# FoX attention in a one-core layer kernel: the small products of a step gathered at one place, the lists of ScalarE and VectorE reordered

## The chip, the cores and the metric

The kernel runs on one core of a Trainium2 chip. A core has five engines that matter here, each with an instruction list of its own that it works through strictly in order: TensorE (PE in the profile, with its weight loader PEld), VectorE (DVE), ScalarE (ACT), GpSimd (POOL) and SyncE (SP), which issues DMA transfers. They wait for one another by semaphores. The metric is the device time of one execution in microseconds (us); the median of three executions before the change is 911.9 us.

## The reference

One layer of a decoder over 528 tokens (16 meta tokens and 512 of the sequence), 1024 features. Cut to what matters:

```python
hn = rms_norm(h_res, norm_mix_gain)
part = lambda i: hn @ w_in[:, o[i]:o[i + 1]]       # q, k, v, fg, glu (2x), gate_attn, gate_conv
# attention, 16 heads of 64, query blocks of 128 that see the keys up to their end:
s = q_block @ k.T / 8 + cum[t] - cum[s]            # cum: running sum of log_sigmoid(fg)
p = softmax(where(causal, s, -inf))
a = (p @ v) @ w_attn_out
# convolution branch:
u = glu[:D] * sigmoid(glu[D:])
c = causal_depthwise_conv(u, conv_dw_w, conv_dw_b)  # 31 taps
c = silu(layer_norm(c)) @ w_conv_out + b_conv_out   # layer_norm over the features
h_res = h_res + (sigmoid(gate_attn) * a + sigmoid(gate_conv) * c) @ w_out
# then a squared-ReLU MLP of 4096 and a last rms_norm; meta tokens are dropped
```

## The kernel before

**Products in three parts.** Every matrix product is done with numbers split in a high and a low part (`w_hi`, `w_lo`, and the same for the input), as three products: high x high, low x high, high x low. A weight chunk is 128 output features times 1024 inputs. SyncE loads it into `raw`, ScalarE copies the high part (`high`, L577), VectorE subtracts to get the low part (`low`, L955), and TensorE runs 24 products of 512 columns (or 24 pairs of 2 x 264 columns where all 528 tokens are wanted, L1451) in `chunk`. There are two places for split chunks, so `low(c + 1)` has to be done before chunk c + 1 starts.

**Pairs of heads.** The stage around the change goes through the projections of q, k, v and the gates, four chunks for each of 8 pairs of heads. It is a loop over k, of 8 steps s = 0 to 7; step s is one half chunk, that is 12 products. In step s of loop k TensorE multiplies the weights of pair k, and beside that does attention for pair k - 1: 8 units, unit s = 4 h + q, for head h of the pair and query block q, with 144, 272, 400 or 528 keys. For a unit the work goes round the engines:

- TensorE: scores S (`unit_scores`, L1571 and L1572), two short products (four for q = 3).
- VectorE: `row_least` (L1091) adds the mask to the scores in PSUM, writes `prob` and finds the row's least value; ScalarE: `exponential` (L666) with the row sum; VectorE: `sum_reciprocal` (L1097); ScalarE: `normalise` (L674).
- TensorE: the transpositions T of P (`unit_transpose`, L1585), q + 2 tiles of 128 x 128 into PSUM. It waits for `normalise` of the unit (`s_pn`) and for all earlier units' `probs_low` (`s_ptl`).
- ScalarE `probs_high` (L682) and VectorE `probs_low` (L1103) take the two parts of the turned P out of PSUM; in the code these calls stand in `turned_out` and `turned_low`, which in step s handle unit s - 2, and in steps 0 and 1 units 6 and 7 of the pair before.
- TensorE: `half_out` (P times v, L1602 and L1605) for two query blocks at once. Then `out_copy` (L689) and `out_high` (L693) on ScalarE, `out_add` (L1110) and `out_low` (L1114) on VectorE. Once a pair TensorE turns v (`values_transpose`, L1613), followed by `values_high` (L735) and `values_low` (L1148).

The evacuations of the projections on ScalarE are in `projection_out` and `second_copy`, on VectorE in `projection_low` (L1141: steps 4 and 6 for the low parts of q and k). VectorE also works off the convolution as single taps of 128 x 512 (`tap`, L1051): the tables `TAPS_FIRST_PAIR` and `TAPS_STEP` say how many taps each of the 8 steps has, and `taps(s, k, a, b)` does those from the a-th to before the b-th of its step. GpSimd adds a finished convolution row to the sum over features (`add_conv`, L552), once the scores of unit 5 are done, in the third to the eighth pair, and at the end twice more, with two memsets (L564, L565) ahead of the last.

**What sets the order.** All lists are written out by hand. In TensorE's `pair_step` the tuple `CUTS` says after how many of the 12 products the small work is put in: S(s) after 4; v's transpositions (step 2) after 7; T(s - 1) after 11, followed by `half_out` in steps 1, 3, 5 and 7.

**The tail.** The loop k = 9 has only the last units and the gates' chunks, together with the layer norm of the convolution: ScalarE and VectorE split the sum over the features (`sum_parts`, L818 and L1248), TensorE's `spread` (L1620, L1621) multiplies both parts with `mean_w` to lay the mean over all partitions, ScalarE copies it to `bc` (L824), VectorE subtracts it from the 8 rows (L1257), ScalarE squares (L829) and VectorE sums the squares (L1239).

## Time and profile before

| what | value |
|---|---|
| runs | 911.46, 911.90, 912.39 us, median 911.90 |
| profiled execution, its own time | 911.48 us |
| its span (first to last instruction) | 909.5 us |
| PE busy | 900.1 us, 99% |
| PEld busy | 784.2 us, 86% |
| DVE busy | 614.1 us, 68% |
| ACT busy | 445.0 us, 49% |
| POOL busy | 22.3 us, 2% |
| mean granted clock of TensorE | 0.999 |
| share of the chain that ended last | PE 92%, DVE 4%, ACT 2%, others 3% |

The profile is of one execution. Its own time is 2.0 us longer than its span, which is what lies before the first and after the last instruction. The pairs of heads take about 134 to 405 us of the span. The shares of busy time are means over the whole span, so a stage has to be looked at by itself: VectorE's 68% are some 95% in the pairs and under half in the MLP. The chain that ended last gives 41% and 17% to the chunk's products (L1455, L1451), 19% to the MLP's (L1707), and 3% each to the transpositions of P and to one form of P times v.

### The profile page before, as it was taken

The numbers are of one execution on the slowest core, as the hardware profiler recorded it, in microseconds if no ns is written. First come the engines' busy times: TensorE is split into PE (matmuls) and PEld (weight loads), VectorE is DVE, ScalarE is ACT, GpSimd is POOL, SyncE is SP. The second block draws the span as 40 slices with busy tenths as digits, with TensorE's granted clock in tenths as the row PEclk, the third lists the DMA queues.
The fourth block names the chain that finished last, engine by engine and source line by source line (L and its number), as shares of the span: only waits on it lengthen the run. The fifth ranks groups of instructions, "written<-read, shape, count | busy, mean of one in ns | idle before, by whom it ended". The sixth has DMA issues, their size and how long they took to land.

```text
span 909.5 us, 13686 instructions
## 1 busy us (share of the span) xinstructions
PE 900.1 (99%) x5039; PEld 784.2 (86%) x5039; DVE 614.1 (68%) x959; ACT 445.0 (49%) x722; POOL 22.3 (2%) x40
## 2 busy tenths in 40 slices
PE   8999999999999999999999999999999999999997
PEld 7999999899999999888888888888888888888886
DVE  7799989999999999987765444533443354334543
ACT  6532246777778777766843244421243133214523
POOL 2010000000000000010000000000000000000000
PEclk9999999999999999999999999999999999999999
DMA  9333332212221222213323532323233333333602
GB/s 267 93 98 92 92 93 70 70 49 70 70 68 48 70 70 54 81 52 92 116 82 104 186 92 85 101 94 100 87 100 108 92 92 92 115 93 98 179 1 93
DMA packets 129466, 84.34 MB, mean 93 GB/s; under 512 B 3103, under 2 KB 118815, under 8 KB 129424
## 3 DMA queue, kind: packets, MB, share of 16 engines
q1 hardware_dynamic: 128192, 82.32, 31.1%
q10 hardware_dynamic: 640, 1.18, 0.4%
q8 instruction: 25, 0.41, 0.2%
q0 software_dynamic: 592, 0.29, 0.2%
q14 instruction: 17, 0.14, 0.1%
HBM read 81.62 MB, written 2.16 MB: 92 GB/s over the span
## 4 chain that ended last, share of the span: by engine, by line
PE 92%; DVE 4%; ACT 2%; issue 1%; DMA 1%; SPq 0%; ACTq 0%
PE pj L1455 41%; PE pQ L1707 19%; PE pj L1451 17%; PE pQ L1585 3%; PE pQ L1602 3%; PE pj L1773 2%; PE pQ L1773 2%; PE pj L1493 1%; DVE cv L1051 1%; PE pQ L1572 1%; PE pQ L1571 1%; DVE w_lo L955 1%; DMA ga<-in_x_dram 1%; ACT w_hi L577 1%; PE pQ L1605 1%
## 5 line engine op out<-in xcount | busy, mean ns | idle before, releaser
L955 DVE TENSOR_TENSOR w_lo<-raw,w_hi 128x1024 fp32r<-128x1024 f32 x129 | 157.6, 1222 | 113.5 <-ACT w_hi L577 113.2
L577 ACT ACTIVATE w_hi<-raw 128x1024 fp32r<-128x1024 f32 x129 | 135.9, 1053 | 161.5 <-PE pQ L1707 121.3
L1455 PE MATMUL pj<-in_hi,w_lo 128*128 128x512 f32 x512 | 201.5, 394 | 0.0
L1455 PE MATMUL pj<-in_lo,w_hi 128*128 128x512 f32 x512 | 200.6, 392 | 0.0
L1455 PE MATMUL pj<-in_hi,w_hi 128*128 128x512 f32 x512 | 200.1, 391 | 0.2 <-DVE w_lo L955 0.2
L1051 DVE SCALAR_TENSOR_TENSOR cv<-u,prm,cv 128x512 f32<-128x512 f32 x240 | 170.6, 745 | 0.5
L1455 PEld LDWEIGHTS pj<-in_hi,w_hi 128*128 128x128 f32 x512 | 96.3, 188 | 19.5 <-DVE w_lo L955 0.6
L1455 PEld LDWEIGHTS pj<-in_lo,w_hi 128*128 128x128 f32 x512 | 96.2, 188 | 17.8
L1455 PEld LDWEIGHTS pj<-in_hi,w_lo 128*128 128x128 f32 x512 | 96.3, 188 | 17.2
L1707 PE MATMUL pQ<-w_hi,mid_hi 128*128 128x512 f32 x256 | 99.8, 390 | 0.0
L1707 PE MATMUL pQ<-w_lo,mid_hi 128*128 128x512 f32 x256 | 99.6, 389 | 0.0
L1707 PE MATMUL pQ<-w_hi,mid_lo 128*128 128x512 f32 x256 | 99.6, 389 | 0.0
L1451 PE MATMUL pj<-in_hi,w_lo 128*128 128x264 f32 x480 | 97.9, 285 | 0.0
L1451 PE MATMUL pj<-in_lo,w_hi 128*128 128x264 f32 x480 | 97.4, 284 | 0.0
L1451 PE MATMUL pj<-in_hi,w_hi 128*128 128x264 f32 x480 | 96.7, 283 | 0.0
L1451 PEld LDWEIGHTS pj<-in_hi,w_hi 128*128 128x128 f32 x480 | 75.1, 188 | 1.0 <-DVE w_lo L955 0.3
L1451 PEld LDWEIGHTS pj<-in_lo,w_hi 128*128 128x128 f32 x480 | 74.1, 188 | 0.0
L1451 PEld LDWEIGHTS pj<-in_hi,w_lo 128*128 128x128 f32 x480 | 74.0, 188 | 0.0
L898 ACT ACTIVATE prob<-pT 128x512 f32<-128x512 f32 x32 | 20.2, 632 | 101.7 <-DVE pT L1348 101.7
L1707 PEld LDWEIGHTS pQ<-w_hi,mid_hi 128*128 128x128 f32 x256 | 48.1, 188 | 10.0
L1707 PEld LDWEIGHTS pQ<-w_hi,mid_lo 128*128 128x128 f32 x256 | 48.1, 188 | 9.9
L1707 PEld LDWEIGHTS pQ<-w_lo,mid_hi 128*128 128x128 f32 x256 | 48.1, 188 | 9.9
(206 smaller groups left out, 1226.1 us busy)
## 6 DMA issues: line engine op xcount, KB each, us to landing
raw<-in_w_in_dram SPq DMA_DIRECT2D x57, 512.0 KB, 3.8
raw<-in_w_mlp_up_dram SPq DMA_DIRECT2D x32, 512.0 KB, 4.0
raw<-in_w_mlp_down_dram SPq DMA_DIRECT2D x32, 512.0 KB, 3.8
raw<-in_w_attn_out_dram SPq DMA_DIRECT2D x8, 512.0 KB, 3.6
raw<-in_w_conv_out_dram SPq DMA_DIRECT2D x8, 512.0 KB, 3.6
raw<-in_w_out_dram SPq DMA_DIRECT2D x8, 512.0 KB, 3.9
ga<-in_x_dram SPq DMA_DIRECT2D x4, 512.0 KB, 8.4
cv<-in_x_dram SPq DMA_DIRECT2D x1, 2048.0 KB, 9.1
```

The costliest lines, as they stand in the source:

```text
L577: A(w_hi[:, c % SPLIT, :], raw[:, c % RAW, :], ACT.Copy).then_inc(s_hi, 1)
L898: A(scratch(j), pT[:, j % 2, :], ACT.Square).then_inc(s_hf, 1)
L955: V.tensor_tensor(w_lo[:, c % SPLIT, :], raw[:, c % RAW, :], w_hi[:, c % SPLIT, :].bitcast(F32), ALU.subtract).then_inc(s_lo, 1)
L1051: V.scalar_tensor_tensor(out=dst, in0=src, scalar=par(j, m), in1=dst, op0=ALU.mult, op1=ALU.add).then_inc(s_conv, 1)
L1451: last = mm(prod(c, T)[:, h * HALF:(h + 1) * HALF], wt, src[:, kt * ROW + FIRST + h * HALF:kt * ROW + FIRST + (h + 1) * HALF], **flags)
L1455: last = mm(prod(c), wt, src[:, at:at + NT], **flags)
L1493: last = mm(prod(c, T)[:, h * HALF:(h + 1) * HALF], (w_hi, w_hi, w_lo)[what][:, c % SPLIT, kt * P:(kt + 1) * P], (in_hi, in_lo, in_hi)[wha ...
L1571: mm(dst[:, a:b], q_a[:, k % 2, h, q * P:(q + 1) * P], k_a[:, k % 2, h, a:b], start=True, stop=False)
L1585: last = nc.tensor.transpose(turned(q)[:, t * P:(t + 1) * P], probs(q, t * P, (t + 1) * P), ident[:, :])
L1602: last = mm(dst.rearrange("p (c n) -> p c n", n=P), v_hl[:, t, h, :], grid[:, first:second + 1:second - first, :], **flags)
L1707: last = mm(y_psum(t, 0), mid[:, tok], w[:, c % SPLIT, cols], start=kt == 0 and n == 0, stop=kt == KT - 1 and n == 2)
L1773: last = mm(y_psum(t, f), hidden[:, tok], w[f][:, cols], start=kt == 0 and n == 0, stop=kt == KT - 1 and n == 2)
```

## The change

On TensorE the small work of a step is gathered: behind the step's first four products come, in this order, T(s - 2) (in steps 0 and 1 that of units 6 and 7 of the pair before), `half_out` in steps 0, 2, 4 and 6, v's transpositions in step 2, and S(s); then the remaining eight products follow without a break. Before, T stood one unit nearer to its scores, eleven products into the step, behind S. The number of tiles and products stays.

On ScalarE and VectorE the calls of a step are put in another order, and the taps are spread over the steps in other numbers with the same total. In the tail, T(7) now stands behind `spread` instead of a step ahead of it, and the layer norm's instructions stand ahead of or behind those of attention in another order. Between `before` and `after` the source lines of ScalarE move by 3, those of VectorE and TensorE by 5 (`probs_low` is L1103 before and L1108 after).

```diff
 TAPS_DONE = (13,) * (KT // 2) + (12,) * (KT // 2)
-TAPS_FIRST_PAIR = (2, 3, 2, 2, 2, 2, 3, 2)
-TAPS_STEP = {18: (3, 4, 1, 2, 1, 2, 3, 2), 19: (3, 4, 1, 2, 2, 2, 3, 2)}
+TAPS_FIRST_PAIR = (3, 4, 2, 2, 1, 3, 1, 2)
+TAPS_STEP = {18: (1, 3, 3, 3, 1, 3, 2, 2), 19: (1, 3, 3, 4, 1, 3, 2, 2)}
...
@@ ScalarE: pair_step
-                if s == 3 and k >= 2:
-                    out_high(k - 2, it)
-                turned_out(s, k, it)
-                if s == 2 and k >= 2:
-                    out_copy(1, k - 2, it)
                 if s == 6:
                     projection_out(s, k, it)
                 if s % 2 == 0 and c > N_PAIR:
                     high(c + 1, it, 8)
+                if s == 2:
+                    if k >= 2:
+                        out_copy(1, k - 2, it)
+                    if live:
+                        values_high(k - 1, it)
+                if s != 6:
+                    turned_out(s, k, it)
+                if s == 3:
+                    projection_out(s, k, it)
+                    if k >= 2:
+                        out_high(k - 2, it)
+                if live:
+                    exponential(s, k - 1, it)
                 if s == 4:
                     projection_out(s, k, it)
-                if s == 3 and k == 1:
-                    projection_out(s, k, it)
+                    second_copy(s, k, it)
+                if s == 6:
+                    turned_out(s, k, it)
                 if live:
-                    exponential(s, k - 1, it)
+                    normalise(s, k - 1, it)
                 if s == 0:
                     projection_out(s, k, it)
-                if s == 2 and live:
-                    values_high(k - 1, it)
-                if s == 3 and k != 1:
-                    projection_out(s, k, it)
-                if s == 6 and live:
-                    out_copy(0, k - 1, it)
-                if s in (4, 6):
+                if s == 6:
                     second_copy(s, k, it)
-                if live:
-                    normalise(s, k - 1, it)
+                    if live:
+                        out_copy(0, k - 1, it)
...
@@ ScalarE: tail, k = 9
                 for s in range(8):
                     c = N_PAIR + 4 * k + s // 2
-                    turned_out(s, k)
-                    if s == 2:
-                        out_copy(1, k - 2)
-                    if s == 3:
-                        out_high(k - 2)
                     if s % 2 == 0:
                         gate_out(s, k)
                         high(c + 1)
                     if s == 0:
                         act.wait_ge(s_csum, KT + 1)
                         A(sum_parts[0], conv_sum[:, :], ACT.Copy).then_inc(s_sumhi, 1)
+                    turned_out(s, k)
+                    if s == 2:
+                        out_copy(1, k - 2)
+                    if s == 3:
+                        out_high(k - 2)
...
@@ VectorE: pair_step
                 if s == 0:
+                    row_least(s, k - 1)
+                    taps(s, k, 0, 1)
+                    turned_low(s, k)
+                    sum_reciprocal(s, k - 1)
+                    low(c + 1)
+                    taps(s, k, 1, None)
+                elif s == 1:
                     taps(s, k, 0, 1)
                     row_least(s, k - 1)
+                    taps(s, k, 1, 2)
                     turned_low(s, k)
-                    taps(s, k, 1, 2)
-                    sum_reciprocal(s, k - 1)
-                    taps(s, k, 2, 3)
-                    low(c + 1)
-                elif s == 1:
-                    turned_low(s, k)
-                    row_least(s, k - 1)
-                    taps(s, k, 0, 2)
                     sum_reciprocal(s, k - 1)
                     taps(s, k, 2, None)
                 elif s == 2:
+                    taps(s, k, 0, 2)
+                    low(c + 1)
+                    row_least(s, k - 1)
+                    values_low(k - 1)
                     turned_low(s, k)
+                    sum_reciprocal(s, k - 1)
+                    taps(s, k, 2, None)
+                elif s == 3:
                     if k >= 2:
                         out_add(1, k - 2)
...
                 elif s == 4:
+                    row_least(s, k - 1)
                     taps(s, k, 0, 1)
                     turned_low(s, k)
+                    sum_reciprocal(s, k - 1)
+                    low(c + 1)
+                    if k < PAIRS:
+                        projection_low(s, k)
+                    taps(s, k, 1, None)
+                elif s == 5:
                     row_least(s, k - 1)
-                    low(c + 1)
+                    taps(s, k, 0, 1)
+                    turned_low(s, k)
                     sum_reciprocal(s, k - 1)
                     taps(s, k, 1, None)
...
-                elif s == 6:
-                    taps(s, k, 0, 3)
-                    row_least(s, k - 1)
-                    turned_low(s, k)
                     if k < PAIRS:
                         projection_low(s, k)
                     sum_reciprocal(s, k - 1)
-                    out_add(0, k - 1)
+                    turned_low(s, k)
+                    taps(s, k, 1, None)
                     low(c + 1)
                 else:
+                    row_least(s, k - 1)
                     turned_low(s, k)
-                    row_least(s, k - 1)
-                    taps(s, k, 0, 1)
+                    out_add(0, k - 1)
                     sum_reciprocal(s, k - 1)
-                    taps(s, k, 1, 2)
+                    taps(s, k, 0, None)
...
@@ VectorE: tail, k = 9
             for s in range(8):
-                turned_low(s, k)
                 if s % 2 == 0:
                     low(N_PAIR + 4 * k + s // 2 + 1)
                 if s == 0:
                     dve.wait_ge(s_sumhi, 1)
                     V.tensor_tensor(sum_parts[1], conv_sum[:, :], sum_parts[0].bitcast(F32), ALU.subtract).then_inc(s_sumlo, 1)
+                turned_low(s, k)
...
@@ TensorE: pair_step
-            CUTS = (0, 4, 7, 11, total // 2)
+            CUTS = (0, 4, total // 2)
...
                     spread(pS[:, 0:NT], sum_parts, s_mu)
+                if s < 2 and k >= 2:
+                    unit_transpose(s + 6, k - 2, it)
+                if s >= 2 and 1 <= k <= PAIRS:
+                    unit_transpose(s - 2, k - 1, it)
+                if s in (0, 2) and k >= 2:
+                    half_out(1, s // 2, k - 2, it)
+                if s in (4, 6) and 1 <= k <= PAIRS:
+                    half_out(0, (s - 4) // 2, k - 1, it)
+                if s == 2 and 1 <= k <= PAIRS:
+                    values_transpose(k - 1, it)
                 if 1 <= k <= PAIRS:
                     unit_scores(s, k - 1, it)
                 chunk(c, at[1], at[2], in_hi, in_lo, width)
-                if s == 2 and 1 <= k <= PAIRS:
-                    values_transpose(k - 1, it)
-                chunk(c, at[2], at[3], in_hi, in_lo, width)
-                if s == 0 and k >= 2:
-                    unit_transpose(7, k - 2, it)
-                if s > 0 and 1 <= k <= PAIRS:
-                    unit_transpose(s - 1, k - 1, it)
-                if s == 1 and k >= 2:
-                    half_out(1, 1, k - 2, it)
-                if s in (3, 5, 7) and 1 <= k <= PAIRS:
-                    half_out(*((0, 0), (0, 1), (1, 0))[(s - 3) // 2], k - 1, it)
-                chunk(c, at[3], at[4], in_hi, in_lo, width)
```

Three places, as the instructions stand in the lists. A row is the line, the operation, the outputs and inputs, the shape, and the semaphores that it waits for; "x2" means twice in a row.

The first place is VectorE's list in the first pair, from the first `low` behind `row_least(0)` on; L955 and L960 are `low`, L1051 and L1056 taps, the rows that write `rinv` are reciprocals, and the 128x256 row that writes `pt_lo` is `probs_low(0)`. Before:

```order
L955 TENSOR_TENSOR w_lo<-raw,w_hi 128x1024 [waits s_hi]
L1091 ISA prob,nmax<-pQ,mask 128x272 [waits s_S]
L1091 ISA nmax 128x1
L1051 SCALAR_TENSOR_TENSOR cv<-u,prm,cv 128x512 [waits s_conv] x2
L1097 RECIPROCAL rinv<-rsum 128x1 [waits s_exp]
L1051 SCALAR_TENSOR_TENSOR cv<-u,prm,cv 128x512 [waits s_conv]
L1103 TENSOR_TENSOR pt_lo<-pQ,pt_hi 128x256 [waits s_pth]
L1091 ISA prob,nmax<-pQ,mask 128x400 [waits s_T,s_S]
L1091 ISA nmax 128x1
```

After:

```order
L960 TENSOR_TENSOR w_lo<-raw,w_hi 128x1024 [waits s_hi]
L1056 SCALAR_TENSOR_TENSOR cv<-u,prm,cv 128x512 [waits s_conv] x3
L1096 ISA prob,nmax<-pQ,mask 128x272 [waits s_S]
L1096 ISA nmax 128x1
L1056 SCALAR_TENSOR_TENSOR cv<-u,prm,cv 128x512 [waits s_conv]
L1102 RECIPROCAL rinv<-rsum 128x1 [waits s_exp]
L1056 SCALAR_TENSOR_TENSOR cv<-u,prm,cv 128x512 [waits s_conv] x4
L960 TENSOR_TENSOR w_lo<-raw,w_hi 128x1024 [waits s_hi]
L1096 ISA prob,nmax<-pQ,mask 128x400 [waits s_T,s_S]
L1096 ISA nmax 128x1
L1153 TENSOR_TENSOR v_hl<-pj,v_hl 128x10x64 [waits s_vh]
L1108 TENSOR_TENSOR pt_lo<-pQ,pt_hi 128x256 [waits s_pth]
```

Before, `probs_low(0)` stood directly behind the taps of step 1 and ahead of `row_least(2)` (128x400); now five more taps, one more `low`, `row_least(2)` and `values_low` (which writes `v_hl`) stand ahead of it.

The second place is VectorE's list in a pair in the middle, from step 4 into step 7, where the 64x512 and 64x528 rows are the low parts of q and k and the row that writes `o_sb` is `out_add`. Before, from `low` in step 4:

```order
L955 TENSOR_TENSOR w_lo<-raw,w_hi 128x1024 [waits s_hi]
L1097 RECIPROCAL rinv<-rsum 128x1 [waits s_exp]
L1141 SCALAR_TENSOR_TENSOR q_a<-pj,q_a 64x512 [waits s_qh] x2
L1091 ISA prob,nmax<-pQ,mask 128x272 [waits s_T,s_S]
L1091 ISA nmax 128x1
L1103 TENSOR_TENSOR pt_lo<-pQ,pt_hi 128x640 [waits s_pth]
L1051 SCALAR_TENSOR_TENSOR cv<-u,prm,cv 128x512 [waits s_conv] x2
L1097 RECIPROCAL rinv<-rsum 128x1 [waits s_exp]
L1051 SCALAR_TENSOR_TENSOR cv<-u,prm,cv 128x512 [waits s_conv] x3
L1091 ISA prob,nmax<-pQ,mask 128x400 [waits s_T,s_S]
L1091 ISA nmax 128x1
L1103 TENSOR_TENSOR pt_lo<-pQ,pt_hi 128x256 [waits s_pth]
```

After, from the low part of q to `probs_low(4)` (128x256):

```order
L1146 SCALAR_TENSOR_TENSOR q_a<-pj,q_a 64x512 [waits s_qh] x2
L1096 ISA prob,nmax<-pQ,mask 128x272 [waits s_T,s_S]
L1096 ISA nmax 128x1
L1056 SCALAR_TENSOR_TENSOR cv<-u,prm,cv 128x512 [waits s_conv]
L1108 TENSOR_TENSOR pt_lo<-pQ,pt_hi 128x640 [waits s_pth]
L1102 RECIPROCAL rinv<-rsum 128x1 [waits s_exp]
L1056 SCALAR_TENSOR_TENSOR cv<-u,prm,cv 128x512 [waits s_conv] x3
L1096 ISA prob,nmax<-pQ,mask 128x400 [waits s_T,s_S]
L1096 ISA nmax 128x1
L1146 SCALAR_TENSOR_TENSOR k_b<-pj,k_a 64x528 [waits s_kh] x2
L1102 RECIPROCAL rinv<-rsum 128x1 [waits s_exp]
L1108 TENSOR_TENSOR pt_lo<-pQ,pt_hi 128x256 [waits s_pth]
```

In step 5, a tap now stands between `row_least(5)` (128x272) and `probs_low(3)` (128x640); in step 6, `probs_low(4)` now stands behind both rows of k's low part instead of directly behind `row_least(6)`.

The third place is VectorE's list at the end of the pairs and the start of the tail; L1248 and L1252 make the low part of the sum for `spread`, L1257 and L1260 subtract the mean. Before:

```order
L1103 TENSOR_TENSOR pt_lo<-pQ,pt_hi 128x384 [waits s_pth]
L1091 ISA prob,nmax<-pQ,mask 128x528 [waits s_T,s_S]
L1091 ISA nmax 128x1
L1051 SCALAR_TENSOR_TENSOR cv<-u,prm,cv 128x512 [waits s_conv]
L1097 RECIPROCAL rinv<-rsum 128x1 [waits s_exp]
L1051 SCALAR_TENSOR_TENSOR cv<-u,prm,cv 128x512 [waits s_conv]
L1103 TENSOR_TENSOR pt_lo<-pQ,pt_hi 128x512 [waits s_pth]
L955 TENSOR_TENSOR w_lo<-raw,w_hi 128x1024 [waits s_hi]
L1248 TENSOR_TENSOR mid_lo<-conv_sum,mid_hi 128x512 [waits s_sumhi]
L1103 TENSOR_TENSOR pt_lo<-pQ,pt_hi 128x640 [waits s_pth]
L1257 TENSOR_TENSOR cv<-cv,bc 128x512 [waits s_mus]
```

After:

```order
L1096 ISA prob,nmax<-pQ,mask 128x528 [waits s_T,s_S]
L1096 ISA nmax 128x1
L1108 TENSOR_TENSOR pt_lo<-pQ,pt_hi 128x384 [waits s_pth]
L1115 TENSOR_TENSOR o_sb<-pQ,o_sb 64x512 [waits s_oa]
L1102 RECIPROCAL rinv<-rsum 128x1 [waits s_exp]
L1056 SCALAR_TENSOR_TENSOR cv<-u,prm,cv 128x512 [waits s_conv] x2
L960 TENSOR_TENSOR w_lo<-raw,w_hi 128x1024 [waits s_hi]
L1252 TENSOR_TENSOR mid_lo<-conv_sum,mid_hi 128x512 [waits s_sumhi]
L1108 TENSOR_TENSOR pt_lo<-pQ,pt_hi 128x512 [waits s_pth]
L1108 TENSOR_TENSOR pt_lo<-pQ,pt_hi 128x640 [waits s_pth]
L1260 TENSOR_TENSOR cv<-cv,bc 128x512 [waits s_mus]
```

Before, the last two taps stood right behind `row_least(7)` (128x528) and around the reciprocal, and both of the last `probs_low` around the sum's low part; now `probs_low(5)`, `out_add` and the reciprocal stand ahead of the two taps, and the last two `probs_low` behind the sum's low part.

## Rows read from the trace of the kernel before

**Rows 1.** Busy time by engine in a stretch of the pairs (columns below).

```profile
core 0: us, PE busy (x) PEld busy (x) DVE busy (x) ACT busy (x) POOL busy (x), PEclk, DMA share, GB/s
200.00:364.00 164.00, 164.00 (x1144) 151.29 (x1143) 155.27 (x314) 122.66 (x241) 8.61 (x9) 1.00 0.23 64
```

**Rows 2.** Waits: engine line <- cause: us in all, times, longest.

```profile
PEld pQ L1585 <- issue: 4.0, 14, 0.9
```

**Rows 3.** Timeline, VectorE, first pair: start, us, engine, line, operation, tiles [idle before].

```profile
138.35 0.31 DVE L1091 CUSTOM_DVE_ANT_0 prob<-pQ,mask 128x144 f32<-128x144 f32 x1
...
139.32 1.21 DVE L955 TENSOR_TENSOR w_lo<-raw,w_hi 128x1024 fp32r<-128x1024 f32 x1
140.44 0.43 DVE L1091 CUSTOM_DVE_ANT_0 prob<-pQ,mask 128x272 f32<-128x272 f32 x1
...
140.80 1.41 DVE L1051 SCALAR_TENSOR_TENSOR cv<-u,prm,cv 128x512 f32<-128x512 f32 x2
...
143.15 0.42 DVE L1103 TENSOR_TENSOR pt_lo<-pQ,pt_hi 128x256 fp32r<-128x256 f32 x1 [0.21 <-ACT pt_hi L682]
...
146.62 0.82 DVE L1148 TENSOR_TENSOR v_hl<-pj,v_hl 128x640 fp32r<-128x640 f32 x1
147.36 0.55 DVE L1103 TENSOR_TENSOR pt_lo<-pQ,pt_hi 128x384 fp32r<-128x384 f32 x1
...
155.97 0.82 DVE L1103 TENSOR_TENSOR pt_lo<-pQ,pt_hi 128x640 fp32r<-128x640 f32 x1
```

**Rows 4.** Timeline, TensorE, first pair.

```profile
144.53 0.49 PE L1585 MATMUL pQ<-ident,prob 128*128 128x128 f32 x3
144.78 0.48 PE L1455 MATMUL pj<-in_hi,w_lo 128*128 128x512 f32 x1
145.09 0.39 PE L1455 MATMUL pj<-in_hi,w_hi 128*128 128x512 f32 x1
...
155.82 0.40 PE L1451 MATMUL pj<-in_lo,w_hi 128*128 128x264 f32 x2
...
156.94 0.41 PE L1585 MATMUL pQ<-ident,prob 128*128 128x128 f32 x2 [0.71 <-DVE pt_lo L1103]
```

**Rows 5.** Timeline, TensorE and VectorE, steps 4 to 7 of a middle pair.

```profile
291.12 0.40 PE L1455 MATMUL pj<-in_lo,w_hi 128*128 128x512 f32 x1
...
296.11 0.39 PE L1455 MATMUL pj<-in_lo,w_hi 128*128 128x512 f32 x1
296.44 0.63 PE L1585 MATMUL pQ<-ident,prob 128*128 128x128 f32 x4
...
285.40 1.41 DVE L1141 SCALAR_TENSOR_TENSOR q_a<-pj,q_a 64x512 fp32r<-64x512 f32 x2
...
291.32 0.57 DVE L1091 CUSTOM_DVE_ANT_0 prob<-pQ,mask 128x400 f32<-128x400 f32 x1
...
292.16 1.43 DVE L1141 SCALAR_TENSOR_TENSOR k_b<-pj,k_a 64x528 fp32r<-64x528 f32 x2
```

**Rows 6.** Timeline, GpSimd and VectorE, end of the last pair.

```profile
395.08 1.29 POOL L552 TENSOR_TENSOR conv_sum<-conv_sum,cv 128x512 f32<-128x512 f32 x1 [8.65 <-DVE cv L1051]
...
395.32 1.61 DVE L1051 SCALAR_TENSOR_TENSOR cv<-u,prm,cv 128x512 f32<-128x512 f32 x1
```

**Rows 7.** Timeline, TensorE and VectorE, last pair and start of the layer norm.

```profile
392.93 0.29 PE L1572 MATMUL pQ<-k_b,q_b 66*128 66x264 f32 x1
...
400.27 0.39 PE L1620 MATMUL pQ<-mid_hi,mean_w 128*128 128x512 f32 x1
...
414.96 0.50 PE L1455 MATMUL pj<-in_hi,w_hi 128*128 128x512 f32 x1 [0.16 <-DVE w_lo L955]
...
393.65 0.69 DVE L1091 CUSTOM_DVE_ANT_0 prob<-pQ,mask 128x528 f32<-128x528 f32 x1
...
394.27 0.73 DVE L1051 SCALAR_TENSOR_TENSOR cv<-u,prm,cv 128x512 f32<-128x512 f32 x1
...
399.31 0.68 DVE L1248 TENSOR_TENSOR mid_lo<-conv_sum,mid_hi 128x512 fp32r<-128x512 f32 x1
...
401.57 1.90 DVE L1257 TENSOR_TENSOR cv<-cv,bc 128x512 f32<-128x512 f32 x3 [0.69 <-ACT bc L824]
```

More of the change, by code:

```diff
@@ L800, in _ @@
                     high(c + 1)
+                if s == 2:
+                    out_copy(1, k - 2)
+                    values_high(k - 1)
+                if s != 6:
+                    turned_out(s, k)
+                if s == 3:
+                    out_high(k - 2)
                 exponential(s, k - 1)
-                if s == 2:
-                    values_high(k - 1)
+                if s == 6:
+                    turned_out(s, k)
                 normalise(s, k - 1)
+                if s == 6:
+                    out_copy(0, k - 1)
             for k in (PAIRS + 1,):
@@ L807, in _ @@
                     c = N_PAIR + 4 * k + s // 2
-                    turned_out(s, k)
-                    if s == 2:
-                        out_copy(1, k - 2)
-                    if s == 3:
-                        out_high(k - 2)
                     if s % 2 == 0:
@@ L818, in _ @@
                         A(sum_parts[0], conv_sum[:, :], ACT.Copy).then_inc(s_sumhi, 1)
+                    turned_out(s, k)
+                    if s == 2:
+                        out_copy(1, k - 2)
+                    if s == 3:
+                        out_high(k - 2)
                     if s == 6:
@@ L1181, in pair_step @@
                 elif s == 2:
+                    taps(s, k, 0, 2)
+                    low(c + 1)
+                    row_least(s, k - 1)
+                    values_low(k - 1)
                     turned_low(s, k)
+                    sum_reciprocal(s, k - 1)
+                    taps(s, k, 2, None)
+                elif s == 3:
                     if k >= 2:
                         out_add(1, k - 2)
+                    taps(s, k, 0, 1)
                     row_least(s, k - 1)
-                    low(c + 1)
+                    taps(s, k, 1, 2)
+                    turned_low(s, k)
                     sum_reciprocal(s, k - 1)
-                    taps(s, k, 0, None)
-                    values_low(k - 1)
-                elif s == 3:
-                    if k == 1:
-                        turned_low(s, k)
-                    row_least(s, k - 1)
-                    if k > 1:
-                        turned_low(s, k)
-                    taps(s, k, 0, 1)
-                    sum_reciprocal(s, k - 1)
-                    taps(s, k, 1, 2)
+                    taps(s, k, 2, None)
                     if k >= 2:
@@ L1201, in pair_step @@
                 elif s == 4:
+                    row_least(s, k - 1)
                     taps(s, k, 0, 1)
                     turned_low(s, k)
+                    sum_reciprocal(s, k - 1)
[4 more added lines that the diff above has]
+                elif s == 5:
                     row_least(s, k - 1)
-                    low(c + 1)
+                    taps(s, k, 0, 1)
+                    turned_low(s, k)
                     sum_reciprocal(s, k - 1)
                     taps(s, k, 1, None)
-                    if k < PAIRS:
-                        projection_low(s, k)
-                elif s == 5:
+                elif s == 6:
+                    taps(s, k, 0, 1)
                     row_least(s, k - 1)
-                    turned_low(s, k)
-                    taps(s, k, 0, None)
-                    sum_reciprocal(s, k - 1)
-                elif s == 6:
-                    taps(s, k, 0, 3)
-                    row_least(s, k - 1)
-                    turned_low(s, k)
                     if k < PAIRS:
@@ L1221, in pair_step @@
                     sum_reciprocal(s, k - 1)
-                    out_add(0, k - 1)
+                    turned_low(s, k)
+                    taps(s, k, 1, None)
                     low(c + 1)
                 else:
+                    row_least(s, k - 1)
                     turned_low(s, k)
-                    row_least(s, k - 1)
-                    taps(s, k, 0, 1)
+                    out_add(0, k - 1)
                     sum_reciprocal(s, k - 1)
-                    taps(s, k, 1, 2)
+                    taps(s, k, 0, None)
             first_step()
@@ L1242, in _ @@
             for s in range(8):
-                turned_low(s, k)
                 if s % 2 == 0:
@@ L1248, in _ @@
                     V.tensor_tensor(sum_parts[1], conv_sum[:, :], sum_parts[0].bitcast(F32), ALU.subtract).then_inc(s_sumlo, 1)
+                turned_low(s, k)
                 if s == 6:
@@ L1253, in _ @@
                     dve.wait_ge(s_mus, 1)
-                if s == 2:
-                    out_add(1, k - 2)
                 for m in CENTRED_AT.get(s, ()):
@@ L1259, in _ @@
                         square_sum(SUMMED_AFTER[m])
+                if s == 2:
+                    out_add(1, k - 2)
                 if s == 3:
```

2 lines of the change are left out of this document (removed).

## The prediction

> **What bounds the kernel now.** I read the busy time by stage first. In the pairs of heads TensorE is busy for the whole of 200 to 364 us, and VectorE for 155.27 of the same 164.00 us [rows 1]. So products set the end, and VectorE, which works through its list strictly in order, has some 5% to spare: a place where TensorE waits for VectorE costs its full length, and a place where it does not costs nothing. The list of waits says how much of that there is before: 14 short waits of the weight loader ahead of the transpositions of P, 4.0 us together [rows 2], and one of 0.71 of TensorE for a `probs_low` [rows 4]. The weight loader runs ahead of the products, so little of the 4.0 us is lost: in a middle pair the products start 296.11 and 296.44 us where 0.23 would do, so 0.10 us is lost there [rows 5]. Then I read the timelines of the first pair, of one middle pair and of the last one, and laid the new lists over them. Durations below are starts to starts where an engine goes straight on, which is 0.06 to 0.09 less than the instruction's own time (a tap takes 0.73 alone, two take 1.41; a `low` of 1.21 has the next instruction 1.12 behind it [rows 3, 7]).
>
> I write T(u), S(u) for the transpositions and the scores of unit u of a pair (u = 0 to 7, q = u mod 4), and step s for the s-th half chunk of TensorE's list.
>
> **The work itself.** The change adds and removes no instruction. On TensorE a block of small products moves, and I cost the moving at nothing: three transpositions and the product behind them take 0.56 us (144.53 to 145.09), of which the tiles start 0.11 apart, the last gives way after 0.03, and the product then takes 0.31 instead of 0.23 [rows 4]. What the block loses on leaving, it gains on its last tile. A step goes from T(s-1) late in step s to T(s-2) early in step s, five products later (some 1.1 us): that is slack for softmax. ScalarE and VectorE keep their totals. So all that is left is waits, at three places.
>
> **First pair: +2.9 us, less 0.9.** VectorE reaches the first `row_least` only at 138.35, without idle time ahead of it, one tap after the last early tap; in the new list that tap stands behind it, so it starts at 137.69 [rows 3]. In the new list there follow, until `probs_low(0)` is done: `row_least(0)` 0.23, nine taps 6.0 (three of step 0, four of step 1, two of step 2), two `low` of 1.12, `row_least(1)` 0.36, two reciprocals 0.07 each, `row_least(2)` 0.50, `values_low` 0.74 and `probs_low(0)` itself 0.42 [rows 3, 5]. That is 10.65, with 0.1 for the second reciprocal's wait on ScalarE 10.75, so it is done at 148.4. T(1) follows 0.15 later, as at 156.94 after 155.97 + 0.82 [rows 3, 4]: 148.55. TensorE gets there earlier: step 3 began at 145.09 with T(1) before it, which now comes after, so at 145.09 - 0.33 = 144.76, and four products of 0.23 later, at 145.7. It waits 2.9 us. Queued behind the wait are S(3) and all products. In the list of before `probs_low(0)` stood at 143.15, ahead of this `low` and of `values_low`. In return the wait at 156.94 goes (155.82 to 156.94 where 0.24 would do: 0.9 us), because TensorE comes 2.9 us later and its T moves five products back [rows 4]. Net **+2.0**; bounds 1.6 to 3.0 (if the 0.9 stays).
>
> **Middle pairs: about +0.3 in all.** Three things.
> Step 7: T(5) waits for `probs_low(4)`, which now stands behind `row_least(6)` and both halves of the key's low part. From `row_least(6)` at 291.32: 0.50, then 1.35 (292.16 to 293.51), reciprocal 0.07, `probs_low(4)` 0.42, and 0.15: T(5) at 293.81. TensorE goes on behind S(6) at 291.12 and has twelve products, 2.74: 293.86 [rows 5]. Margin 0.05, so 0 to 0.1 a pair.
> Step 6: T(4) waits for `probs_low(3)`. By the same addition (from S(4): 0.23, tap 0.67, 0.60, 0.07, `low` 1.12, query's low part 1.44, `row_least(5)` 0.37, tap 0.67, `probs_low(3)` 0.82 and 0.19 of signals, 6.2 against 6.4 of TensorE [rows 3, 5]) the margin is about 0.25. But a tap now stands right behind `row_least(5)`, and that is where GpSimd starts `add_conv`, which waits for S(5). One row shows what a tap does beside it: GpSimd's addition ran 395.08 to 396.37, and the tap of 395.32 took 1.61 instead of 0.73, to 0.56 after the addition's end [rows 6]. Before, step 5 had `row_least` and `probs_low(3)` there, which read PSUM, and the taps came when the addition was over. Six pairs have such an addition. `row_least(5)` comes 0.45 after S(5), since VectorE is still at the query's low part, so the tap starts 0.7 into a window of 1.3 and loses some 0.4: 0.4 - 0.25 = 0.13 a pair. From 0 (tap after the window) to 0.6 (tap at its start).
> The Trainium skill, "SBUF — State Buffer", section "Who interferes with whom", says that a VectorE instruction with two SBUF inputs contends with a GpSimd instruction that reads SBUF, and that whichever issues first holds the shared ports for the whole instruction. The row of 395.32 agrees; by the rule alone, with the tap at the window's start in all six pairs, the sum would be 3 us higher.
> Gains: T(6) and T(4) of before lose 0.1 each or less [rows 5], some 0.14 a pair. Sum: 6 x 0.13 + 7 x 0.05 - 7 x 0.14 = 0.15; I take **+0.3**, bounds -1.3 and +3.5.
>
> **Last pair and layer norm: +2.4.** TensorE's `spread` product of the mean waits for the low part of the summed convolution, behind the last two taps. Before, it came at 400.27, with that part done at 399.31 + 0.68: just in time [rows 7].
> (a) In the new step 7 VectorE does `row_least(7)` (from S(7)'s end, 392.93 + 0.29, so 393.26), `probs_low(5)`, `out_add(0)` (a subtraction of 512 columns takes 0.68 in a row of its own), the reciprocal and only then both taps: 0.62 + 0.47 + 0.60 + 0.08, so the first tap starts at 395.0 instead of 394.27 [rows 3, 7]. From that tap to the end of the low part the old chain through GpSimd, ScalarE and VectorE took 5.72 (394.27 to 399.99); the new one ends at 400.75, up to 0.3 sooner or later by how the second tap and GpSimd's first addition meet, and `spread` follows 0.15 behind, at 400.9. TensorE comes T(7) sooner, at 400.27 - 0.55 = 399.7. It waits 0.9 to 1.5: I take 1.2. Queued behind it: T(7) and all products.
> (b) T(7) then stands behind `spread` and `probs_low(6)` behind the low part: another 0.15.
> (c) Before, the mean went straight from `spread` (400.27) to the centring at 401.57, 1.30 later. Now T(7) and its two copies on ScalarE and VectorE go between: T(7) starts 0.61 after `spread` and ends at 1.32, ScalarE's copy 0.75, VectorE's 0.74: the centring starts 2.84 after `spread`, 1.54 later, while TensorE itself loses 0.70 by T(7). VectorE's list from there to the weight split that TensorE waited 0.16 for at 414.96 keeps its length, so that wait grows by 0.84, plus up to 0.5 where ScalarE's squares queue behind `out_high`, which now waits for a later `out_add(1)`: 1.0.
> Sum 1.2 + 0.15 + 1.0 = **2.35**; bounds 1.4 and 3.3.
>
> **Sum.** 2.0 + 0.3 + 2.35 = 4.65 us. The profiled execution took 911.48 us, so 916.1; the median of the runs is 911.9, 0.4 above it, so **916.6**.
>
> **Rivals.**
> 1. Breaks in the stream of products cost (the other side). Before, a pair has 17 places where small products interrupt the chunk (eight S, eight T, one of v), now eight. If each cost the 0.08 by which the product after T is longer [rows 4], 9 x 0.08 x 8 pairs = 5.8 us come back, and 4.65 of waits leave -1.1: 910.8, faster by 0.1%; from 0.09 a break on it would be faster by 0.2% (910.1). Against: the last tile's 0.03 in the same rows gives the 0.08 back. 5%.
> 2. All the 4.0 us of the loader's waits [rows 2] are real loss and go: 911.9 + 4.65 - 3.9 = 912.6, no change. Against: products lost 0.10 where the loader idled 0.3. 7%.
> 3. Only the first pair costs, because TensorE, once late, leaves VectorE its slack to the end: 911.9 + 2.0 = 913.9. For: VectorE has 5% idle. Against: the tail's chain is VectorE's and GpSimd's own, and starts from S(7). 12%.
> 4. The tap meets GpSimd's addition at its start in all six pairs: +3 us, 919.6. For: the row of 395.32. Against: the query's low part delays `row_least(5)`. 10%.
> 5. The wait of 2.9 us lets TensorE's clock fall. The granted clock is 1.00 in every stretch I read, also in 200 to 364 [rows 1], and no row has products at the lower level; at half the rate for as long as the wait lasted, 1.5 to 3 us more: 919. 5%. The Trainium skill, "TensorE: Matmul & The Clock Gate", section "What's actually happening", says that an engine which was idle gets the lower of its two clocks; nothing in the pairs shows it yet.
>
> **How the numbers follow.** The forecast has 61%: its terms end at 2.0 + 0.3 + 2.35 with their bounds, most of it between 914.3 and 919. With rivals 3, 4 and 5 in part, the range is 913.9 to 919.7. Below it lie rivals 1 and 2 (12%), above it what is left of 4 and 5. About 0.2%, 1.8 us, is what a measurement of this kernel can tell from no change: faster 0.05, same 0.08, slower 0.87.
>
> **What would show it.** First pair: an idle time of 2.5 to 3 us of TensorE or its loader ahead of the second T, ended by VectorE's `probs_low`, near 148 us, and none of 0.7 a step and a half later. Middle pairs: taps of 1.0 to 1.3 us behind `row_least(5)` in six pairs, and idle times of 0.1 to 0.3 us ahead of T(4) and T(5). Tail: about 1.2 us ahead of `spread` and 1.2 ahead of the seventh chunk of the gates. It is wrong if TensorE's idle time in the first pair is under 1 us, which would mean that VectorE's list is not what binds there, or if the pairs of the middle grow or shrink by more than 0.4 us each, which would mean a cost or gain in the products themselves.

## The result and the profile after

The changed kernel takes 918.22 us (median of 6 runs, 916.98 to 919.47) against 911.82 before: 1.0067 times as long, 95% interval 1.0057 to 1.0078, that is 6.4 us slower. The profiled execution took 918.51 us, with a span of 916.5 and a mean granted clock of 0.996 (before: 911.48, 909.5 and 0.999).

The list of waits of after (engine, line waited for, cause: us in all, times, longest) answers to [rows 2]: three waits of TensorE are new or longer, and the loader's waits ahead of T have nearly doubled, from 4.0 to 7.8, most of the growth in one of 3.1.

```profile
PEld pQ L1590 <- issue: 7.8, 15, 3.1
PE pQ L1590 <- DVE pt_lo L1108: 2.7, 1, 2.7
PE pQ L1625 <- DVE mid_lo L1252: 1.6, 1, 1.6
PE pj L1460 <- DVE w_lo L960: 1.4, 1, 1.4
```

**First pair** (timeline of after: start, us, engine, line; VectorE, then TensorE), answering to [rows 3, 4]:

```profile
146.88 0.58 DVE L1096 CUSTOM_DVE_ANT_0 prob<-pQ,mask 128x400 f32<-128x400 f32 x1
147.37 0.83 DVE L1153 TENSOR_TENSOR v_hl<-pj,v_hl 128x640 fp32r<-128x640 f32 x1
148.11 0.42 DVE L1108 TENSOR_TENSOR pt_lo<-pQ,pt_hi 128x256 fp32r<-128x256 f32 x1
...
145.55 0.39 PE L1460 MATMUL pj<-in_hi,w_hi 128*128 128x512 f32 x1
148.68 0.87 PE L1590 MATMUL pQ<-ident,prob 128*128 128x128 f32 x3 [2.74 <-DVE pt_lo L1108]
149.20 0.57 PE L1576 MATMUL pQ<-k_a,q_a 128*128 128x264 f32 x1
...
150.23 0.63 PE L1460 MATMUL pj<-in_lo,w_hi 128*128 128x512 f32 x1
150.65 0.63 PE L1460 MATMUL pj<-in_hi,w_lo 128*128 128x512 f32 x1
...
151.93 0.40 PE L1460 MATMUL pj<-in_hi,w_lo 128*128 128x512 f32 x1
152.18 0.39 PE L1460 MATMUL pj<-in_hi,w_hi 128*128 128x512 f32 x1
```

T(1) waits 2.74 us for `probs_low(0)`; from the start of the product ahead of it to its own pass 3.13 us, 2.9 more than the usual 0.23. And what follows it is slow: products stand 0.42 apart until 151.93 and take 0.63, then 0.25 and 0.40. The stretches of the trace (busy us of PE, PEld, DVE, ACT, POOL, then granted clock, DMA share and GB/s) show why:

```profile
145.00:148.90 3.90, 1.16 (x6) 0.69 (x5) 3.90 (x9) 1.56 (x5) 0.00 (x0) 0.95 0.11 24
148.90:152.00 3.10, 3.10 (x12) 2.71 (x12) 1.88 (x5) 2.14 (x5) 0.00 (x0) 0.51 0.47 139
```

The granted clock is 0.51 there, the lower of TensorE's two levels (1.2 instead of 2.4 GHz).

**Middle pairs**, the pair of [rows 5]: GpSimd's addition, VectorE's tap beside it, and TensorE's T(4):

```profile
290.56 1.29 POOL L552 TENSOR_TENSOR conv_sum<-conv_sum,cv 128x512 f32<-128x512 f32 x1 [23.80 <-PE pQ L1577]
...
291.39 1.01 DVE L1056 SCALAR_TENSOR_TENSOR cv<-u,prm,cv 128x512 f32<-128x512 f32 x1
292.32 0.81 DVE L1108 TENSOR_TENSOR pt_lo<-pQ,pt_hi 128x640 fp32r<-128x640 f32 x1
...
292.94 0.40 PE L1460 MATMUL pj<-in_hi,w_hi 128*128 128x512 f32 x1
293.28 0.41 PE L1590 MATMUL pQ<-ident,prob 128*128 128x128 f32 x2
```

The tap takes 1.01 instead of 0.73 in five pairs, and 1.52 in the sixth; T(4) starts 0.34 behind the product ahead of it where 0.23 would do.

**Tail** (VectorE, GpSimd, TensorE), answering to [rows 7]:

```profile
399.05 1.39 DVE L1056 SCALAR_TENSOR_TENSOR cv<-u,prm,cv 128x512 f32<-128x512 f32 x2
...
404.52 0.69 DVE L1252 TENSOR_TENSOR mid_lo<-conv_sum,mid_hi 128x512 fp32r<-128x512 f32 x1 [1.84 <-ACT mid_hi L818]
...
408.21 1.89 DVE L1260 TENSOR_TENSOR cv<-cv,bc 128x512 f32<-128x512 f32 x3
...
399.85 1.75 POOL L552 TENSOR_TENSOR conv_sum<-conv_sum,cv 128x512 f32<-128x512 f32 x1 [9.77 <-DVE cv L1056]
...
402.17 1.65 POOL L552 TENSOR_TENSOR conv_sum<-conv_sum,cv 128x512 f32<-128x512 f32 x1
...
405.26 0.50 PE L1625 MATMUL pQ<-mid_hi,mean_w 128*128 128x512 f32 x1 [1.59 <-DVE mid_lo L1252]
...
421.96 0.50 PE L1460 MATMUL pj<-in_hi,w_hi 128*128 128x512 f32 x1 [1.35 <-DVE w_lo L960]
```

`spread` waits 1.59, and the seventh chunk of the gates 1.35 instead of 0.16. GpSimd's two additions take 1.75 and 1.65 instead of 1.30.

### The profile page after: what moved, and what is told of

Its sections match the earlier page's. It is cut to its first block, busy times and chain, and to the rows that moved or that the text cites. A ratio compares the mean times of both kernels' runs of the same rounds, so it can differ in the third digit from the quotient of the medians.

```text
span 916.5 us, 13695 instructions
## 1 busy us (share of the span) xinstructions
PE 901.6 (98%) x5039; PEld 784.9 (86%) x5039; DVE 615.3 (67%) x959; ACT 450.1 (49%) x722; POOL 23.1 (3%) x40
## 4 chain that ended last, share of the span: by engine, by line
PE 92%; DVE 4%; ACT 1%; issue 1%; DMA 1%; POOL 0%; POOLq 0%; SPq 0%; ACTq 0%
PE pj L1460 40%; PE pQ L1710 19%; PE pj L1456 17%; PE pQ L1590 3%; PE pQ L1607 3%; PE pj L1776 2%; PE pQ L1776 2%; DVE cv L1056 2%; PE pj L1498 1%; PE pQ L1577 1%; PE pQ L1576 1%; DVE w_lo L960 1%; DMA ga<-in_x_dram 1%; PE pQ L1610 1%; PE pj L1509 0%
## 5 line engine op out<-in xcount | busy, mean ns | idle before, releaser
L960 DVE TENSOR_TENSOR w_lo<-raw,w_hi 128x1024 fp32r<-128x1024 f32 x129 | 157.6, 1222 | 113.2 <-ACT w_hi L577 112.9
L1056 DVE SCALAR_TENSOR_TENSOR cv<-u,prm,cv 128x512 f32<-128x512 f32 x240 | 172.6, 753 | 0.7
```

What stands on the lines that cost most here:

```text
L960: V.tensor_tensor(w_lo[:, c % SPLIT, :], raw[:, c % RAW, :], w_hi[:, c % SPLIT, :].bitcast(F32), ALU.subtract).then_inc(s_lo, 1)
L1056: V.scalar_tensor_tensor(out=dst, in0=src, scalar=par(j, m), in1=dst, op0=ALU.mult, op1=ALU.add).then_inc(s_conv, 1)
```

## Experiments: one stage at a time

The theory: the 6.4 us are three separate debts, in the first pair, the middle pairs and the tail, and each is VectorE's order. The main rivals: a debt is made up for by later slack, or it comes from TensorE's new order itself. The kernel before was timed again beside each group of runs: 911.90 us beside e_first, e_last, e_both and e_warm, 911.69 beside e_early, e_table, e_pe and e_lists, and 911.64 beside the others. Small differences between runs of different groups are taken against these.

**e_first** undoes the first pair: for k = 1 the steps of before on three engines.

```diff
-TAPS_FIRST_PAIR = (3, 4, 2, 2, 1, 3, 1, 2)
+TAPS_FIRST_PAIR = (2, 3, 2, 2, 2, 2, 3, 2)
...
-                    pair_step(s, k)
+                    (old_step if k == 1 else pair_step)(s, k)
...
```

The last two lines stand in ScalarE's and in VectorE's list; TensorE's list has the old places for k = 1 in a block of its own.

> The kernel after, with the first pair of heads (k = 1) as in the kernel before on all three engines: T(s-1) late in the step, the old lists of ScalarE and VectorE, the old row of taps; everything from the second pair on is as after. If the first pair costs what its trace shows (2.7 us of wait ahead of T(1), some 1.5 us of products at half rate behind it, less the 0.9 us that the old list lost there): 914.8 us. If only the wait counts and the half rate has another cause: 916.4. If the later pairs had made up for the wait anyway: 917.5 to 918.2.

Measured: 914.92 us (914.75 to 915.01), mean clock 0.998 to 1.000. The first pair costs 3.3 us. Between the two profiled executions (918.51 and 914.99) it is 3.5, which is what the trace of after adds up to (2.9 of wait and 1.5 of half rate, less the old 0.9), so no later slack gives any of it back.

**e_last** does the same for k = 8 and the tail k = 9.

> The kernel after, with the last pair (k = 8) and the layer norm's tail (k = 9) as in the kernel before on all three engines. If the tail costs what I read from its trace (the wait ahead of spread, T(7) behind it, and the later wait for the weight split, about 3.2 us together): 915.1 us. If what it loses is given back by waits behind it: 917.5 to 918.2.

Measured: 915.39 us. The last pair and the tail cost 2.8 us. All three engines are as before there, so this run does not tell which of the moved instructions costs what; that is read from the traces alone.

**e_both** undoes both.

> First pair, last pair and tail as before, the pairs 2 to 7 as after. What is left over the kernel before is the change in the middle pairs alone. My theory: about +0.3 us, 912.1 (911.6 to 912.8), with a tap slowed by GpSimd in step 5 of the pairs. Rival, gathering the small products saves their breaks: below 911.0. Rival, the new lists make TensorE wait in every pair: above 913.

Measured: 911.93 us against 911.90 of before (ratio 1.0000, 0.9991 to 1.0009). The middle pairs together cost nothing that the time can show. The trace is finer: from the first product of pair 2 to that of pair 8, TensorE falls behind the kernel before by 0.36 us here and by 0.31 in after. Other kernels with these same middle pairs (e_first, e_last, e_warm, e_early, e_table) fall behind by 0.18 to 0.26, so a single trace is good for about 0.1 us.

## Experiments: the wait and the clock

**e_warm** keeps the wait but gives TensorE something to do in it:

```diff
+                if k == 1 and s == 3:
+                    for _ in range(11):
+                        mm(pO7[:, 0:NT], w_hi[:, c % SPLIT, 0:P], in_hi[:, FIRST + META:FIRST + META + NT],
+                           start=True, stop=True)
                 if s >= 2 and 1 <= k <= PAIRS:
                     unit_transpose(s - 2, k - 1, it)
```

> The kernel after with 11 more products of 512 columns (2.5 us; w_hi with in_hi, into the part of PSUM that P times v uses later) ahead of T(1) in the first pair: they fill the wait and change no result. If the idle time is what lets TensorE's clock fall to its lower level: no product at half rate behind T(1), mean clock 0.999, and 916.7 us in spite of 2.5 us more work. If the half rate comes from the burst of transpositions and scores, or from the transfers that start then: half rate as before, 918.2. If the added products delay T(1): above 918.5.

Measured: 917.01 us (916.89 to 917.41) with 2.5 us more work, 1.2 less than after. Its timeline (TensorE), and then its stretches:

```profile
145.67 2.65 PE L1656 MATMUL pQ<-in_hi,w_hi 128*128 128x512 f32 x11
148.56 0.52 PE L1590 MATMUL pQ<-ident,prob 128*128 128x128 f32 x3 [0.24 <-DVE pt_lo L1108]
...
150.35 0.39 PE L1460 MATMUL pj<-in_hi,w_lo 128*128 128x512 f32 x1
```

```profile
145.00:148.90 3.90, 3.66 (x19) 2.80 (x17) 3.90 (x9) 1.56 (x5) 0.00 (x0) 1.00 0.14 35
148.90:152.00 3.10, 3.10 (x20) 2.74 (x19) 2.15 (x6) 2.48 (x6) 0.00 (x0) 1.00 0.42 126
```

T(1) comes at the same time, but the clock stays at 1.00, although nearly the same transfers run (126 GB/s against 139), and the same transpositions and scores: from T(1) to the fifth product behind it takes 1.79 us instead of 3.25 in the profiled execution of after. So the idle time is what the clock fell for, and 1.5 us is its price in that execution. The price does not seem to be the same in each: the six of after have mean clocks from 0.995 (919.47 us) to 0.999 (916.98), those of e_warm 0.998 to 0.999.

**e_early** tests whether one misplaced instruction makes the wait:

```diff
                 elif s == 2:
+                    if k == 1:
+                        turned_low(s, k)
                     taps(s, k, 0, 2)
                     low(c + 1)
                     row_least(s, k - 1)
                     values_low(k - 1)
-                    turned_low(s, k)
+                    if k > 1:
+                        turned_low(s, k)
...
```

> The kernel after, with probs_low(0) moved to the front of step 2 in VectorE's list of the first pair, and nothing else moved. Theory that VectorE as a whole is behind in the first pair (it comes from the early taps without idle time): T(1) no longer waits, but row_least(2) and what stands behind it come as late as before, so S(3) waits for it some 2.6 us instead, the products behind it run at half rate as in after, and the time stays at 918.2, within 0.6. Rival, that the place of probs_low(0) alone is the cause: both the wait and the half rate go, 914.9 or less.

Measured: 918.65 us (917.27 to 921.07), no gain. TensorE's timeline:

```profile
146.08 0.52 PE L1593 MATMUL pQ<-ident,prob 128*128 128x128 f32 x3 [0.17 <-DVE pt_lo L1108]
148.94 0.39 PE L1579 MATMUL pQ<-k_a,q_a 128*128 128x264 f32 x1 [2.34 <-DVE nmax L1096]
```

The wait has only moved on, from T(1) to S(3), which now waits for `row_least(2)`. In this profiled execution (917.27) the clock stayed up in the wait and behind it:

```profile
145.00:150.00 5.00, 2.49 (x13) 1.69 (x13) 4.43 (x9) 1.33 (x5) 0.00 (x0) 1.00 0.04 6
150.00:154.00 4.00, 4.00 (x28) 3.44 (x27) 2.31 (x6) 3.74 (x8) 0.00 (x0) 1.00 0.45 128
```

So the half rate that I expected did not come in the one execution that has a trace; longer executions of the same kernel have mean clocks down to 0.994 (921.07).

**e_table** changes only numbers:

```diff
-TAPS_FIRST_PAIR = (3, 4, 2, 2, 1, 3, 1, 2)
+TAPS_FIRST_PAIR = (1, 0, 3, 5, 0, 5, 0, 4)
```

> The kernel after with another row of taps for the first pair, (1, 0, 3, 5, 0, 5, 0, 4) instead of (3, 4, 2, 2, 1, 3, 1, 2): the same 18 taps, six fewer of them ahead of probs_low(0), the orders as in after. Theory that VectorE is only late there, and has the time for these taps in the steps behind: no wait of over 0.3 us in the first pair, full rate throughout, and the 0.9 us that the kernel before lost there are gone too: 914.0 (913.6 to 914.9). Rival, that the taps cost the same wherever they stand in this pair: a wait of 1 to 3 us in steps 4 to 7, 916 to 918.2.

Measured: 914.15 us. The list of waits has no TensorE wait for a `probs_low` any more, and its loader's longest ahead of T is 0.4:

```profile
PEld pQ L1590 <- issue: 4.7, 14, 0.4
```

The granted clock is 1.00 from 134 to 200 us. The order of the calls and the gathered place are those of after, so neither has to be undone in the first pair: VectorE comes into it late, and taking six taps out from ahead of `probs_low(0)` removes the wait. Whether fewer than six would do was not tried.

## Experiments: the two parts alone, and the repairs

**e_pe** and **e_lists** are the two halves of the change:

```diff
# e_pe: the block of TensorE of after, all else of before
# e_lists: the block of TensorE of before, all else of after
```

> TensorE's list of after with the lists of ScalarE, VectorE and the tables of before: one part of the change alone. If the gathered place on TensorE by itself costs nothing and the new lists bring the loss: 911.9 or less. If the lists were made for the old places: the old lists copy out v and the low parts too late for the chunks, some 0.8 us in most pairs and 2.5 in the tail, 919 to 920.

> TensorE's list of before with the lists of ScalarE, VectorE and the tables of after: the other part alone. In the new lists a probs_low stands a step later, while T of the next unit still stands at its old place: by adding the durations up TensorE waits 0.3 to 1.4 us at five or six places of every pair, 6 us a pair, 950 to 965. If the new lists are only a little worse than the old: 912 to 916.

Measured: 919.35 and 962.87 us. In the list of waits of e_pe, chunks wait for ScalarE's copy of v out of PSUM, and `spread` for the low part of the convolution's sum:

```profile
PE pj L1451 <- ACT vT L702: 3.8, 6, 0.6
PE pQ L1620 <- DVE mid_lo L1248: 1.3, 1, 1.3
```

In that of e_lists, T waits for a `probs_low` 39 times:

```profile
PE pQ L1590 <- DVE pt_lo L1108: 36.5, 39, 3.8
```

The halves belong together. Against the kernel before, e_lists loses 51 us. e_pe loses 7.7, and after 6.4: that is no clear difference, since the times of after spread over 2.5 us, but TensorE's half alone is no gain either, and its waits are others.

**e_swap** is e_both with `probs_low(3)` ahead of the tap again in step 5:

```diff
                     row_least(s, k - 1)
-                    taps(s, k, 0, 1)
                     turned_low(s, k)
+                    taps(s, k, 0, 1)
                     sum_reciprocal(s, k - 1)
```

> As e_both (first pair, last pair and tail as before, pairs 2 to 7 as after), with one more change: in step 5 probs_low(3) stands ahead of the tap again, behind row_least(5). If the tap that meets GpSimd's addition is what the middle pairs lose: no tap over 0.8 us beside an addition in pairs 3 to 7, and TensorE does not fall behind from pair 2 to pair 8 (in e_both it fell back 0.36 us from chunk to chunk in the trace): 911.6. If the middle pairs lose at T(5) behind the low part of k instead: 911.9, and TensorE falls back as in e_both.

Measured: 910.86 us (ratio 0.9991, 0.9982 to 1.0000). Against the kernel before of its own group that is 0.8 less, where e_both was equal to it: more than the 0.3 that I expected. The tap now comes behind the addition and takes 0.74, and T(4) follows the product ahead of it by 0.23:

```profile
287.90 0.82 DVE L1158 TENSOR_TENSOR pt_lo<-pQ,pt_hi 128x640 fp32r<-128x640 f32 x1
288.64 0.74 DVE L1106 SCALAR_TENSOR_TENSOR cv<-u,prm,cv 128x512 f32<-128x512 f32 x1
...
289.46 0.39 PE L1577 MATMUL pj<-in_hi,w_hi 128*128 128x512 f32 x1
289.69 0.38 PE L1707 MATMUL pQ<-ident,prob 128*128 128x128 f32 x2
```

From pair 2 to pair 8 TensorE now gains 0.46 us on the kernel before instead of losing 0.36. The tap beside the addition thus costs 0.82, or 0.14 in each of six pairs. With the spread of single traces named above it is 0.6 to 0.8.

**e_comb** puts the repairs together: the taps of e_table, last pair and tail of before, step 5 of e_swap. **e_new_best** is e_comb with VectorE's calls and rows of taps in the pairs ordered once more, **e_old_best** the same for the kernel before, with its places on TensorE.

> All repairs on the kernel after: the row of taps of e_table in the first pair, last pair and tail as before, step 5 as in e_swap; TensorE's gathered place stays in pairs 1 to 7. By the sum of the single runs (918.2 - 4.1 for the first pair - 2.8 for the tail - 0.3) 911.0, so 0.1% below the kernel before. If the gains overlap (a TensorE that is less late makes the next wait longer): 911.8 or more.

> As e_comb, with VectorE's lists in all pairs ordered anew so that by the durations of the trace no T waits at all. If waits for VectorE are all that is left to gain in this stage: 910.6 to 911.2. If a lower bound is set by TensorE's own products: not below 911, as e_comb.

> The kernel before with its places on TensorE, and VectorE's lists and taps ordered anew so that by the durations of the trace no T waits, the 0.9 us of the first pair among them. If gathering the small products were worth something in itself, this would stay above e_new_best by more than 0.3 us; my theory is that the place is worth nothing where no engine is late: the same time, 910.7 to 911.2.

Measured: 910.26 (ratio 0.9984, 0.9975 to 0.9993), 910.93 and 910.32 us (0.9985, 0.9976 to 0.9994), against 911.64 of before. Two of them are faster than the kernel before, by 0.15%: e_comb, with the gathered place in pairs 1 to 7, and e_old_best, with the old one throughout. Their lists on VectorE differ as well, so this does not test the place by itself. e_comb is 0.7 below the sum that I gave, since that counted e_swap at 0.3 and not at 0.8. e_new_best is 0.7 slower than e_comb: T still waits in three of its pairs, at 194.83, 227.85 and 260.85 us, and starts there some 0.3 late each, counted from the start of the product ahead of it.

## Why the prediction came out as it did

The forecast was 916.6 and slower, in a range from 913.9 to 919.7; measured are 918.22, slower. The direction, the three places and the waits there were right. One term was put at nothing, and one was too small.

- **First pair, 2.9 less 0.9.** T(1) was forecast at 148.55 and came at 148.68; the forecast wait of 2.9 is 2.9 from start to start, and the old wait of 0.71 [rows 4] is gone. This sum of VectorE's list was right. What the forecast lacked is the clock: rival 5, with 5%, came in part. Two of the six executions have a mean clock of 0.998 or 0.999, and take 917.0, near the forecast; the median has some 1.2 more, and e_warm says the same. The step that failed is that "no row has products at the lower level" was taken as a reason against, when no wait of TensorE in the trace of before is as long as the one that I forecast (the longest is 1.47, ahead of its first product). That trace does show the fall, but outside of the rows that I read: TensorE's last product starts at 903.40 us, and from 908.0 to 909.5 the granted clock is 0.50.
- **Middle pairs, +0.3.** In the trace 0.31. The parts hold too: 6 x 0.13 was forecast for the tap beside GpSimd's addition, and e_swap against e_both gives 0.82 (0.4 less 0.25 is 0.15 and not 0.13, a slip of 0.1 in all). The rest of the new order was put at a gain of 0.63 (0.98 less 0.35); it is 0.46.
- **Tail, 2.35.** e_last gives 2.8. The waits came where they were forecast: `spread` 1.59 (forecast 1.2), the seventh chunk 1.35 (0.16 and 1.0); ahead of the latter, as forecast, ScalarE's `out_high` waits for the later `out_add(1)`, 2.74 instead of 0.97. The term that was too small is (a): I let the old chain of 5.72 us start later and gave it 0.3 either way, but GpSimd's additions in it grew by 0.45 and 0.35, as the second tap and then a `low` were on VectorE when they began; 0.3 came back, as the low part of the sum no longer stood behind a `low`. So from the first tap to the end of that low part the chain took 6.16 (399.05 to 405.21).
- **Rivals.** 1 fell in its size: its 0.72 a pair would be 4.3 us from pair 2 to pair 8, where e_comb, gathered, is 0.17 shorter than e_old_best, with the old places and hardly a wait. A saving of that smaller size is not excluded. 2 fell: the loader's waits ahead of T did not go (4.0 before, 5.3 in e_both), and e_old_best, with 3.5 of them, is level with the fastest kernel. 3 fell: e_first, without the first pair's loss, is still 3.0 slower than before. 4 did not come in five of six pairs: the tap met the addition 0.83 after its start (290.56 and 291.39), forecast 0.7. In the sixth it met it 0.32 after, and took 1.52.

The rule from the Trainium skill on the ports that VectorE and GpSimd share ("SBUF — State Buffer", "Who interferes with whom") is borne out both ways in these rows: where GpSimd was first, the tap grew from 0.73 to 1.01; where VectorE was first, the addition grew from 1.30 to 1.75. The rule from the Trainium skill, "TensorE: Matmul & The Clock Gate", "What's actually happening", that an idle engine gets the lower clock, is borne out by after against e_warm, while e_early's profiled execution had a wait of 2.34 with no fall behind it.

## What to carry to other kernels

An engine that works in order and is nearly full has to be added up from the point where it comes in late, instruction by instruction, up to the one that is waited for; here, moving that one instruction ahead only moved the wait, and taking work out from ahead of it (six taps) removed it. If the sum forecasts a wait of TensorE longer than any in the profile, give a chance to a stretch of products at half rate behind it, and look for something useful that TensorE can do in the meantime: the filler of e_warm did 2.5 us more work and was still 1.2 us faster than after. Places on one engine and lists on the others are one design: the new lists alone were 51 us slower than the kernel before, and the new places alone 7.7.

## What the runs showed of the hardware

In the traces TensorE's granted clock falls to 0.50 or 0.51 in four waits, of 2.69 (e_last), 2.74 (after), 3.58 and 3.84 us (both e_lists, ahead of 448.23 and 148.80), and stays at 1.00 behind those of 2.34 (e_early), 1.59 and 1.35 (the tail of after). These are the stretches of e_last with its wait and behind it:

```profile
145.00:148.90 3.90, 1.21 (x7) 0.73 (x6) 3.90 (x9) 1.56 (x5) 0.00 (x0) 0.95 0.12 29
148.90:152.00 3.10, 3.10 (x12) 2.71 (x11) 1.88 (x5) 2.13 (x5) 0.00 (x0) 0.51 0.44 132
```

The loss does not seem to be the same in each execution: the times of after lie 2.5 us apart (916.98 to 919.47, mean clocks 0.999 to 0.995) and those of e_early 3.8 us, while those of e_first, e_warm, e_table and e_comb, which have no such idle time there, lie within 0.3 to 0.9 us. Yet e_last, with the same idle time as after (2.69, then a clock of 0.51), lies within 0.34 us (915.24 to 915.58). In the profiled execution of after (918.51) the clock falls once and is 1.00 again from 152 us to the last product. Whether the longest execution loses its clock a second time, behind the wait of `spread`, or longer at the first place, and whether the shortest do not lose it at all, stays open: only one execution of each kernel has a trace.

Of an addition on GpSimd and a tap on VectorE the one that came second was slowed (the tap from 0.73 to 1.01 or 1.52 us, the addition from 1.30 to 1.75), so a tap that is moved can delay a chain on GpSimd that does not appear in the change at all.
